# A two-block network on one core: the post norms of the second block go through PSUM, the output is turned tile by tile, and the layer loop is written out

## The reference

```python
def rms_norm_2(x, gain):
    x32 = x.astype(jnp.float32)
    y = x32 * lax.rsqrt(jnp.mean(x32 * x32, axis=-1, keepdims=True) + RMS_EPS)
    return (y * gain.astype(jnp.float32)).astype(x.dtype)

def second_block(x, attn_pre_norm, w_in, ..., ffn_post_norm):
    for i in range(DEPTH):                                   # DEPTH = 2
        h = rms_norm_2(x, attn_pre_norm[i])
        z = h @ w_in[i]
        ...                                                  # attention, convolution, gated delta rule -> mix
        x = x + rms_norm_2(mix @ w_out[i], attn_post_norm[i])
        h = rms_norm_2(x, ffn_pre_norm[i])
        f = (jax.nn.silu(h @ w_gate[i]) * (h @ w_up[i])) @ w_down[i]
        x = x + rms_norm_2(f, ffn_post_norm[i])
    return x
```

## Time and profile before

| | us |
|---|---|
| median of 3 runs | 2900.07 (2896.43 to 2901.28) |
| the profiled execution | 2899.27 |
| its span in the trace | 2897.5 |

### The profile page before, as it was taken

The page is one execution under the profiler, slowest core; times in us unless marked ns, Lnnn a source line. Parts: engine busy times, 40 slices in busy tenths (PEclk is TensorE's granted clock), DMA queues, the critical chain, the costliest instruction groups (busy, mean ns, idle before and its releaser), DMA issues.

```text
span 2897.5 us, 37049 instructions
## 1 busy us (share of the span) xinstructions
PE 2660.6 (92%) x11991; PEld 2109.7 (73%) x12001; DVE 1655.6 (57%) x2106; ACT 1061.5 (37%) x1433; POOL 106.0 (4%) x94
## 2 busy tenths in 40 slices
PE   6999999999999999989878799999899698799995
PEld 4657888887578888866668588887566596588884
DVE  4555755645557557457875644343668774643445
ACT  3654433435544334322513332222224324422322
POOL 0000000000000000002010100000101100100001
PEclk9999999999999999999989899999899899899997
DMA  3202333332023323421200133333112101233331
GB/s 107 79 1 74 100 102 88 104 101 75 8 64 96 109 87 102 113 61 52 66 1 1 58 87 104 91 97 93 51 51 59 37 1 30 65 97 99 94 103 63
DMA packets 403449, 208.20 MB, mean 72 GB/s; under 512 B 9762, under 2 KB 401380, under 8 KB 403332
## 3 DMA queue, kind: packets, MB, share of 16 engines
q1 hardware_dynamic: 397546, 203.24, 24.3%
q0 software_dynamic: 1696, 1.61, 0.3%
q10 hardware_dynamic: 4090, 1.89, 0.3%
HBM read 205.56 MB, written 2.10 MB: 72 GB/s over the span
## 4 chain that ended last, share of the span: by engine, by line
PE 85%; DVE 8%; issue 3%; ACT 3%; ACTq 0%; DVEq 0%; DMA 0%; another core or an unknown queue 0%
PE ps L535 61%; PE ps L554 8%; PE ps L997 2%; PE ps L1012 1%; PE ps L748 1%; PE ps L1008 1%; ACT lnt L1160 1%; PE ps L876 1%; PE ps L899 1%; PE ps L891 1%; DVE cv L2264 1%; PE ps L723 1%; DVE mx L1796 1%; PE ps L863 0%; DVE yc L2069 0%
## 5 line engine op out<-in xcount | busy, mean ns | idle before, releaser
L1156 ACT ACTIVATE whi<-raw 128x1024 fp32r<-128x1024 f32 (+1 forms) x354 | 395.9, 1118 | 1198.0 <-PE ps L535 1108.3
L535 PE MATMUL ps<-h_hi,whi 128*128 128x512 f32 x1920 | 767.8, 400 | 1.1 <-issue 1.1
L535 PE MATMUL ps<-h_lo,whi 128*128 128x512 f32 x1920 | 753.2, 392 | 0.0
L535 PE MATMUL ps<-h_hi,wlo 128*128 128x512 f32 x1920 | 513.5, 389 | 1.6 <-DVE wlo L1694 1.6
L1694 DVE TENSOR_TENSOR wlo<-raw,whi 128x1024 fp32r<-128x1024 f32 (+1 forms) x354 | 458.3, 1295 | 24.8 <-ACT whi L1156 23.6
L535 PEld LDWEIGHTS ps<-h_hi,whi 128*128 128x128 f32 x1920 | 364.4, 190 | 82.8 <-issue 4.0
L535 PEld LDWEIGHTS ps<-h_lo,whi 128*128 128x128 f32 x1920 | 364.2, 190 | 80.3 <-issue 4.3
L535 PEld LDWEIGHTS ps<-h_hi,wlo 128*128 128x128 f32 x1920 | 360.2, 188 | 77.2 <-DVE wlo L1694 2.4
L535 PE MATMUL ps<-a_hi,whi 128*128 128x512 f32 x752 | 295.3, 393 | 3.0 <-DVE a_lo L2218 2.7
L535 PE MATMUL ps<-a_lo,whi 128*128 128x512 f32 x752 | 293.2, 390 | 0.0
L2283 DVE TENSOR_TENSOR cv<-ps,rstd 128x512 f32<-128x512 f32 x88 | 60.8, 691 | 248.8 <-PE ps L535 241.0
(11 more groups left out here) (342 smaller groups left out, 3295.3 us busy)
## 6 DMA issues: line engine op xcount, KB each, us to landing
raw<-in_w_up SPq DMA_DIRECT2D x132, 512.0 KB, 3.8
raw<-in_w_down SPq DMA_DIRECT2D x64, 704.0 KB, 4.5
raw<-in_w_in SPq DMA_DIRECT2D x82, 512.0 KB, 3.8
raw<-in_w_gate SPq DMA_DIRECT2D x44, 512.0 KB, 3.8
raw<-in_w_o SPq DMA_DIRECT2D x16, 512.0 KB, 3.6
raw<-in_w_out SPq DMA_DIRECT2D x16, 512.0 KB, 3.6
xs<-in_x SPq DMA_DIRECT2D x1, 2048.0 KB, 8.2
out<-xs SPq DMA_DIRECT2D x8, 256.0 KB, 2.0
```

The source lines that it names most:

```text
L535: return pe.matmul(ps[:, ACC[s], :], w[s][:, k, :], r[:, k, :], start=start, stop=stop)
L1156: act.activation(whi[s][:, 0:kt, :], raw[s][:, 0:kt, :], ACT.Copy).then_inc(w_hi_ready.sem, 1)
```

## The change

Six edits, all in the second block:

1. **PSUM between the two DVE steps.** ACT writes the post norm's scale to the PSUM bank `TRN[0]` and DVE its scaled y to `ROT[n % 2]`, in place of `cv[0]` and of `cv[1]` or `prod` in SBUF.
2. **Low halves shared.** DVE makes those of tiles 0, 2, 4, 6, 7. For tiles 1, 3, 5 ACT also writes x times gain in f32 to `pad`, and POOL subtracts `h_hi` from it.
3. **Sum of squares shared.** POOL adds tiles 0 to 5; tiles 6 and 7 stay in `sqt` and go to PE, so the sum over channels takes three matmuls (`post_norm_sum`). ACT does `h_hi` before the square, except for tile 7. Likewise the last square of y goes to PE directly (`post_sum`), and ACT makes it before its last `hi_next`.
4. **`stream_pair`** takes the place of `first_pair` behind three of the post norms: both units for each tile as it comes, six matmuls for tiles 0 to 4, five for 5 to 7, three at the end.
5. **The output** is turned one tile (128 channels, all tokens) at a time as soon as that x is there, copied by ACT, and stored in five transfers; the last post norm makes no halves and no squares.
6. **The layer loop** of the second block is written out in Python on PE, ACT, DVE and POOL (SP keeps its loop; it now waits for `rstd` and not for the last `h_lo` before it loads the gate weights).

```diff
-        ysq_ready, yssq_done = sem("ysq_ready", 2 * KD), sem("yssq_done", 2 * KD)
+        ysq_ready, yssq_done = sem("ysq_ready", 2 * KD), sem("yssq_done", 2 * (KD - 1))
...
+        LOW_DVE, LOW_POOL = (0, 2, 4, 6, 7), (1, 3, 5)
...
-                        sp.wait_ge(h_ready.sem, h_ready.at(L * 2 + 2 * DEPTH, KD - 1))
+                        sp.wait_ge(rstd_ready.sem, rstd_ready.at(L * 2 + 2 * DEPTH, 0))
...
-            for hf in range(2):
-                for tb in range(TB):
-                    sp.wait_ge(out_kept.sem, hf * TB + tb + 1)
...
+            STORES = ((0, 2), (2, 4), (4, 6), (6, 7), (7, 8))
+            for n0, n1 in STORES:
+                sp.wait_ge(out_kept.sem, n1)
+                sp.dma_start(out[0].rearrange("(t p) d -> p t d", p=P)[:, :, n0 * P:n1 * P],
+                             xs[:, :, n0 * P:n1 * P]).then_inc(out_stored.sem, 16)
...
+            def post_low(p, i):
+                n = LOW_POOL[i]
+                pool.wait_ge(pxg_ready.sem, pxg_ready.at(p, i))
+                pool.wait_ge(phhi_ready.sem, phhi_ready.at(p, n))
+                nc.gpsimd.tensor_tensor(h_lo[:, n, :], pad[i % 2][:, 0:SEQ], h_hi[:, n, :].bitcast(F32),
+                                        ALU.subtract).then_inc(plo_pool.sem, 1)
...
+            def post_parts(p):
+                post_low(p, 0)
+                post_square_sum(p, 1)
+                post_square_sum(p, 2)
+                post_low(p, 1)
+                post_square_sum(p, 3)
+                post_square_sum(p, 4)
+                post_low(p, 2)
+                post_square_sum(p, 5)
...
+            def stream_pair(v, rhs_hi, rhs_lo, wait_rhs, before_last):
...
+                for k in range(KD):
+                    if k == KD - 1:
+                        before_last()
+                    wait_rhs(k, 0)
+                    for s in range(2):
+                        product(k, s, whi, rhs_hi, start=k == 0)
+                        product(k, s, whi, rhs_lo)
+                        if s == 0 or k < KD - 3:
+                            mm = product(k, s, wlo, rhs_hi, stop=s == 0 and k == KD - 1)
...
+                for k in range(KD - 3, KD):
+                    mm = product(k, 1, wlo, rhs_hi, stop=k == KD - 1)
...
-            with pe.Fori(0, DEPTH) as L:
+            for L in range(DEPTH):
...
-            for hf in range(2):
-                pe.wait_ge(x2_ready.sem, x2_ready.at(DEPTH - 1, KD + 4 * hf + 3))
+            for n in range(KD):
+                pe.wait_ge(x2_ready.sem, x2_ready.at(DEPTH - 1, KD + n))
+                if n >= 2:
+                    pe.wait_ge(out_kept.sem, n - 1)
...
+                    def square(n):
+                        if n >= 2:
+                            act.wait_ge(pssq_done.sem, pssq_done.at(p, max(n - 3, 0)))
+                        act.activation(sqt[:, n % 2, :], x[:, n, :], ACT.Square).then_inc(psq_ready.sem, 1)
...
+                    for n in range(KD):
+                        act.wait_ge(x2_ready.sem, x2_ready.at(L, i * KD + n))
+                        if n < KD - 1:
+                            high(n)
+                            square(n)
+                        else:
+                            square(n)
+                            high(n)
...
-                            scaled = (cv[1], prod)[n % 2]
-                            order.step(dve.scalar_tensor_tensor(scaled[:], y[:, n, :], gain(L * 2 * KD + ((GENS + i) * KD + n)), cv[0][:],
+                        scaled = ps[:, ROT[n % 2], :]
+                        order.step(dve.scalar_tensor_tensor(scaled, y[:, n, :], gain(L * 2 * KD + ((GENS + i) * KD + n)), ps[:, TRN[0], :],
...
+                        order.told(dve.tensor_tensor(x[:, n, :], x[:, n, :], scaled, ALU.add), x2_ready, L, i * KD + n)
+                        if more and n - 1 in LOW_DVE:
+                            post_low(n - 1)
```

More of the change, by code:

```diff
@@ L809, in _ @@
                             unit(V + OFF_DOWN[hf] + j, s, HALF, a_hi, a_lo, need_a)
[L812 removed]
+            for L in range(DEPTH):
                 V = BASE2 + L * PAIRS2
                 G = L * 2 + 2 * DEPTH
[L815 removed]
+                need_in = need_h(G) if L == 0 else need_post(2 * L - 1)
+                if L == 0:
+                    first_pair(V, h_hi, h_lo, need_in, range(KD - 2), range(KD - 2, KD), (KD - 1, lambda: norm_sum(G)))
+                else:
+                    stream_pair(V, h_hi, h_lo, need_in, lambda: post_norm_sum(2 * L - 1))
                 def gate_columns():
@@ L911, in _ @@
                 for i in range(2, N_IN2):
-                    unit(V + i // 2, i % 2, KD, h_hi, h_lo, need_h(G))
+                    unit(V + i // 2, i % 2, KD, h_hi, h_lo, need_in)
                     if i - 2 < 2 * NA:
@@ L1112, in _ @@
                 post_sum(0)
-                first_pair(V + OFF_UP2[0], h_hi, h_lo, need_h(G + 1), range(KD - 2), range(KD - 2, KD), (KD - 1, lambda: norm_sum(G + 1)))
+                stream_pair(V + OFF_UP2[0], h_hi, h_lo, need_post(2 * L), lambda: post_norm_sum(2 * L))
                 for hf in range(2):
@@ L1116, in _ @@
                         for s in range(2):
-                            unit(V + OFF_UP2[hf] + j, s, KD, h_hi, h_lo, need_h(G + 1))
+                            unit(V + OFF_UP2[hf] + j, s, KD, h_hi, h_lo, need_post(2 * L))
                     def need_a2(k, s, hf=hf):
@@ L1431, in _ @@
                     drain(PAIRS_DOWN - 1, KD)
-            with act.Fori(0, DEPTH) as L:
+            for L in range(DEPTH):
                 V = BASE2 + L * PAIRS2
@@ L1617, in _, with post_square @@
                 order.restart()
+                def post_square(i, v, j, s):
+                    act.wait_ge(acc_free.sem, v * 2 + (s + 3))
+                    n = j * 2 + s
+                    if not (isinstance(j, int) and j == 0):
+                        act.wait_ge(yssq_done.sem, yssq_done.at(L, i * (KD - 1) + n - 2))
+                    act.activation(cv[s][:], tile(y, n), ACT.Square).then_inc(ysq_ready.sem, 1)
                 def post_squares(i, v, j, hi_kt):
@@ L1622, in post_squares, with last_post_squares, post_rstd @@
                         hi_next(v + 1, s, hi_kt)
[L1623 to L1629, removed]
+                        post_square(i, v, j, s)
+                def last_post_squares(i, v):
+                    hi_next(v + 1, 0, KD)
+                    post_square(i, v, PAIRS_O - 1, 0)
+                    post_square(i, v, PAIRS_O - 1, 1)
+                    hi_next(v + 1, 1, KD)
+                def post_rstd(i):
                     logs_and_exps()
@@ L1956, in _ @@
                         order.restart()
-            with dve.Fori(0, DEPTH) as L:
+            for L in range(DEPTH):
                 V = BASE2 + L * PAIRS2
@@ L2246, in branch @@
                             continue
+                        if isinstance(n, int) and n == KD - 1:
+                            low(v + 1, s, kt)
+                            continue
                         dve.wait_ge(ysq_ready.sem, ysq_ready.at(L, i * KD + n))
```

127 lines of the change are left out of this document (81 added, 46 removed).

## The result

| | before | changed |
|---|---|---|
| median, us | 2899.34 (2896.43 to 2901.28, 4 runs) | 2852.89 (2851.62 to 2854.59, 4 runs) |
| ratio | 1 | 0.9841, interval 0.9824 to 0.9858 |
| profiled execution | 2899.27 | 2854.59 |
| its span | 2897.5 | 2852.8 |

A forecast was written before the change was run, and what follows sets the result against it. PE, busy 92% of the span, bounds the kernel, so gains come only where it stands still, around four post norms. Terms 5.9 + 7.2 + 5.9 + 17.4 + 8 = 44.4 from 2899.27 give 2854.9 us, range 2842 to 2870.

The forecast's parts named there:

- DVE waits for POOL only with two inputs in SBUF: Post norms: POOL costs nothing to L2382 and L2385 with one SBUF input; low halves with two take the full wait.
- The lock rival: Post norms: PSUM forms wait for POOL too, 0.96 for each of eight steps, 7.7 in three places: 2878; chance 0.04.
- PSUM writes cost nothing: DVE steps writing PSUM: 0 taken, bounds 0.06 either way over 16 steps in four places, 4 us; chance of bound 0.05.
- The sum of a post norm: First post norm, DVE's first step to PE's full units: 21.7 instead of 29.25, gain 5.9 after 1.5 for the clock.
- PE's three sums (1.02 for one now) are done before: End of a post norm: PE's sums over channels finish before ACT's table load ends at 18.95, so they add nothing.
- the low-clock rival: Post norms: PE stays at 1.2 GHz, gains only 1.35, 3.2, 1.35; 13.1 worse, 2868; chance 0.14.
- The 1.5 put down to the clock: Three post norms: PE's clock may fall back in gaps before tiles 5 and 7, costing 1.5 us a place.
- POOL is the late one now: Post norm: POOL's last sum ends at 16.3, after DVE is done with x 7 at 13.7.
- The layers written out: Second block's layer loop: 35 DVE or ACT steps a layer save 0.11 each, 8 us; bounds 0 and 14.
- The slow rival: Longer program makes inner loop turns wait for instructions, 52 x 1.83 = 95 us, 2950; chance 0.03.
- SP's later load of the gate weights: SP waits for rstd, so gate weights come some 5 us later; hidden, or 5 us a layer with no cover.
- The output: Last post norm to the end: 16.2 us from DVE's first step instead of 33.65, gain 17.4.

The follow-up runs named there:

- e4: Changed kernel with the post norm's scale and scaled y put back in SBUF (cv[0], cv[1], prod); 2872.44 us, ratio 0.9914.
- e1: Changed kernel with PE's three sums over channels made ahead of tile 6's matmuls instead of tile 7's; 2850.51 us, ratio 0.9833.
- e8: Changed kernel with first_pair (unit 0, then unit 1) in place of stream_pair behind the three post norms; 2865.83 us, ratio 0.989.
- e10: Changed kernel with all low halves on DVE, POOL only summing five squares; 2857.08 us, ratio 0.9858.
- e5: Kernel before with only the second block's layer loop written out on PE, ACT, DVE and POOL; 2890.95 us against 2898.75, ratio 0.9975.
- e2: Changed kernel without ACT's second load of the logarithm and exponential table ahead of rstd; 2853.12 us.
- e3: Changed kernel with the sums ahead of tile 6 and without the second table load ahead of rstd; 2849.12 us.
- e7: Changed kernel with the output turned by halves as before, copied by ACT, stored in eight pieces of 256 KB; 2854.94 us, ratio 0.9854.
- e9: Kernel of e3 with POOL making the low half of tile 5 before its sum of tile 4; 2847.55 us, ratio 0.9822.

## Why the prediction was right, point by point

- **The total.** From the profiled execution 44.4 were forecast and 44.7 came, but with the first block's 3.3 us of scatter taken out it is 48.0. The fronts gave 10.5 where 8 were forecast, the three norms 20.4 for 19.0, the output 17.5 for 17.4. That the total agrees to 0.3 is luck.
- **DVE waits for POOL only with two inputs in SBUF.** Right, and shown both ways: L2385 at 0.69 with PSUM, 1.63 without it (e4). The lock rival is out. It was priced at 7.7 a place and e4 shows 5.6: eight steps of DVE are held up by 1.0 each there, about as priced, but its low halves then take 0.74 and lose nothing, where the changed kernel's lose 2.4 in that place (1.24, 1.89 and 1.51). The Trainium skill, SBUF — State Buffer, in Who interferes with whom, has both sides as a rule: a VectorE instruction with two inputs in SBUF contends with a GpSimd instruction that reads SBUF, and one with at most one such input, outside the two-port modes, doesn't. The traces agree: 1.63 and 1.78 in e4, 0.69 and 0.75 in the changed kernel.
- **PSUM writes cost nothing.** Right: the step that writes PSUM takes 0.75 in the changed kernel and 0.75 in e4. The table of the Trainium skill, VectorE: DVE Perf Modes, in its section on the TRN2 errata, has PSUM to SBUF 62 cycles longer; here a step with an input in PSUM takes 686 ns in the median (L2385) and one with both in SBUF 692 (e4, where POOL is idle), so the measurement decides against it.
- **The sum of a post norm.** 23.0 from DVE's first step to PE's full units (1644.12 to 1667.14), where 21.7 and 1.5 for the clock, 23.2, were forecast. **The size was right and its reason wrong.** The step that failed is "PE's three sums (1.02 for one now) are done before". They were not: they begin at 1661.67, behind tile 6, and end 0.86 apart, which holds the logarithm back by 2.00. The main line named three sums and the 1.02 of one, but gave them no place in PE's queue and no time there; only the low-clock rival had them in PE's line. In the second place it is the same: 23.9 (2020.73 to 2044.60), where 22.4 and 1.5 were forecast, and again 2.00 of waiting for the sums. The 1.5 put down to the clock was not spent there: after its rise at 1653.5 PE's records of a product stay at 0.39 (more only behind a pause or a sum), and e1, which moves the sums alone, takes 1.5, 1.8 and 1.5 back. The window's granted clock is 0.79 in the mean, just under the 0.8 that the forecast named as its sign.
- **Two smaller errors off the path.** x of tile 7 was forecast at 13.7 and came at 14.8 (1658.93), since the low halves of tiles 2 and 4, which stand ahead of it, took 1.24 and 1.89. POOL's last sum was forecast at 16.3 and ended at 15.7. "POOL is the late one now" is true of the last square (ACT waits 1.08 for POOL), but that square ends at 16.4 and PE's sums begin only at 17.6.
- **The low clock.** This rival did not come. e8 is the nearest to it: there the clock stays low until 1663.3 and the three places are 11.3 worse together, near the 13.1 that the rival had, though part of it is the order. The reason given against it, that PE has next to no pause in the first half, is what the rows show. One of its terms is too small: it has 2.7 for the three sums at the lower clock, and the one such sum that a trace shows takes 1.71 by itself (e10). The Trainium skill, TensorE: Matmul & The Clock Gate, in HAM oscillation, tells of a clock that falls back where bursts are short against the waits. In e8 there is no fall, the clock was not up yet (0.64 in the mean, with a pause at each tile); e10 has one, but behind pauses of 0.4 to 0.9 between bursts of 1.5, so it isn't that case either.
- **The layers written out.** 8 forecast, 7.8 measured by e5, 8.4 in its two fronts. The size is right, its working only in part: 35 steps a layer at 0.11 were counted, and the chain of a front lost 25 pieces, 2.6 us a layer by the estimate above. The changed kernel's second front gained 2 more than e5's. The loop is written out in both, and the records of PE there are longer in e5 (323.8 in all, 319.6 in the changed kernel), which speaks for the clock, as below. The slow rival of 1.83 for each inner turn did not appear: the run of 480 matmuls takes 109.1, and took 108.95 before.
- **SP's later load of the gate weights** costs nothing. They are used in a layer's front, by the products at L892 (L823 before), and these start 19.26 us after the second layer's first full unit (2063.86), where it was 19.23 (2078.55).
- **The output.** 16.2 from DVE's first step (2836.63) to the end, 16.2 forecast. Inside, the last x was 11.2 and came at 11.2 (2847.83), the last turn began at once, the copy took 0.60.

## What to carry to other kernels

Where VectorE and GpSimd work side by side, look at which steps have two inputs in SBUF: with one of them in PSUM the step here took 0.69 and not 1.63, and that was worth 16.8 us in three short stretches. When work moves to a further engine, write that engine's queue out as well, with every instruction that it gains and what stands ahead of it: a step that "is done before" has to be placed, not assumed. And feed TensorE in few large bursts while it waits: the same 48 matmuls, ordered so that there are six to a tile and not three, got the higher clock ten us earlier (e8).

## What the runs showed of the hardware

- **The same code can get a different clock.** The front of the second layer took 369.1 to 369.8 in seven kernels (the changed one, e1, e2, e3, e7, e8, e10), 371.5 in e4 and 373.4 in e9, with the same code; the first front took 368.8 to 369.2 in all of these. In e9 a few matmuls behind the transposes of the second layer run at 1.2 GHz (0.63 a record):

```profile
2071.27 1.12 PE L900 MATMUL ps<-ident,probs 128*128 128x128 f32 x4 [2.70 <-DVE probs L2213]
2072.04 0.78 PE L560 MATMUL ps<-h_hi,whi 128*128 128x512 f32 x1
2072.61 0.63 PE L560 MATMUL ps<-h_lo,whi 128*128 128x512 f32 x1
```

and the same place in e3 does not, after the same pause of 2.70:

```profile
2074.49 0.66 PE L900 MATMUL ps<-ident,probs 128*128 128x128 f32 x4 [2.70 <-DVE probs L2213]
2074.90 0.47 PE L560 MATMUL ps<-h_hi,whi 128*128 128x512 f32 x1
```

  So a few us of a gain can be given back or added in code that the change does not touch; a term of 2 us is better read from its own stretch than from the total. What sets it is open, and with one profiled execution of each kernel it is also open whether it belongs to the kernel or to the execution.
- **A sum in plain f32 is dear.** `ones` by 128x512 f32 takes 0.86 from start to start at the higher clock, where a product takes 0.23. Three of them weigh as much as eleven products.
- **GpSimd pays too.** Beside VectorE's steps with two SBUF inputs its own take 1.47 to 1.74 in the first place of e4, where they take 1.3 in the changed kernel. So both engines lose time to the wait.

Not tried: the sum of squares given back to POOL alone, and SP's load after the last `h_lo`; what each is worth by itself is open, though the gate products, where the second would show, have not moved.
